# A three-block sequence kernel: convolution fed in narrower units, the S5 recurrence moved to VectorE, the last section taken token tile by token tile

## The reference, cut to what matters

```
# second block, x: (512, 1024), u = rms_norm(x) * g
a, a_z, b_val, b_gate, b_z = split(u @ ev_w_in)          # each (512, 1024)
# S5: 64 groups of 16 channels, 64 complex states each
s_t = Lbar * s_{t-1} + Bbar u_t ;  y_t = Re(C s_t) + D u_t
ya  = gelu(y);  ya = ya * sigmoid(ya @ w_glu + b) * silu(a_z)
# conformer convolution, 31 taps, causal, depthwise
h   = b_val * sigmoid(b_gate)
h   = silu(layer_norm(conv31(h)))
yb  = (h @ w_pw + b_pw) * silu(b_z)
x   = x + rms_norm([ya, yb] @ ev_w_out)
# third block (GLA), end of it
y   = sum over 4 heads of o_h @ od_w_out[h]              # (512, 1024)
out = x + rms_norm(y)
```

## Time and profile before

| | |
|---|---|
| median of 3 runs | 1820.9 us (1819.47 to 1821.16) |
| profiled execution, its own time | 1818.73 us |
| span in the profile | 1817.0 us |
| TensorE (PE) busy | 1680.5 us, 92% |
| VectorE (DVE) busy | 1005.8 us, 55% |
| ScalarE (ACT) busy | 610.4 us, 34% |
| GpSimd (POOL) busy | 296.3 us, 16% |
| mean granted TensorE clock | 0.969 |

### The profile page before, as it was taken

The page is one execution under the profiler, slowest core; times in us unless marked ns, Lnnn a source line. Parts: engine busy times, 40 slices in busy tenths (PEclk is TensorE's granted clock), DMA queues, the critical chain, the costliest instruction groups (busy, mean ns, idle before and its releaser), DMA issues.

```text
span 1817.0 us, 20356 instructions
## 1 busy us (share of the span) xinstructions
PE 1680.5 (92%) x7876; PEld 1364.0 (75%) x7876; DVE 1005.8 (55%) x1271; ACT 610.4 (34%) x852; POOL 296.3 (16%) x316
## 2 busy tenths in 40 slices
PE   6999989999999999989977876999989999999995
PEld 5887878878888888879955656768877777787764
DVE  4375254552345244547999979965454344354434
ACT  4333322233212233343411214255245244243431
POOL 4980000000000000030199284200000000000000
PEclk9999999999999999999988898999999999999998
DMA  8556433233333322263312231115313122131211
GB/s 243 131 146 161 118 103 94 93 116 109 100 93 98 100 93 99 76 232 93 117 35 58 70 139 47 47 64 170 105 47 93 59 82 92 46 105 57 70 47 58
DMA packets 129467, 177.39 MB, mean 98 GB/s; under 512 B 50683, under 2 KB 61419, under 8 KB 128363
## 3 DMA queue, kind: packets, MB, share of 16 engines
q1 hardware_dynamic: 127563, 173.62, 30.9%
q10 hardware_dynamic: 1664, 2.13, 0.4%
q0 software_dynamic: 160, 0.52, 0.2%
HBM read 161.58 MB, written 14.68 MB: 97 GB/s over the span
## 4 chain that ended last, share of the span: by engine, by line
PE 76%; DVE 19%; ACT 2%; issue 1%; POOL 1%; SPq 0%; DMA 0%; ACTq 0%; DVEq 0%; POOLq 0%
PE PS L1960 67%; DVE TMP L1639 8%; DVE WL L1295 2%; PE PS L1938 2%; PE PS L2210 1%; PE PS L2228 1%; DVE FIX L1676 1%; DVE S L1678 1%; PE PS L2081 1%; PE PS L2219 1%; ACT XN L901 1%; DVE V L1373 1%; DVE SEGV L1610 1%; DVE S L1621 1%; DVE S L1618 1%
## 5 line engine op out<-in xcount | busy, mean ns | idle before, releaser
L1960 PE MATMUL PS<-HH,WH 128*128 128x512 f32 x1216 | 485.4, 399 | 46.5 <-DVE WL L1295 35.5
L1295 DVE TENSOR_TENSOR WL<-WR,WH 128x1024 fp32r<-128x1024 f32 x200 | 256.3, 1289 | 466.3 <-ACT WH L896 466.2
L1960 PE MATMUL PS<-HL,WH 128*128 128x512 f32 x1216 | 479.8, 395 | 0.0
L1960 PE MATMUL PS<-HH,WL 128*128 128x512 f32 x1216 | 479.3, 394 | 0.0
L896 ACT ACTIVATE WH<-WR 128x1024 fp32r<-128x1024 f32 x200 | 210.7, 1059 | 709.1 <-PE PS L1960 695.7
L1960 PEld LDWEIGHTS PS<-HH,WH 128*128 128x128 f32 x1216 | 232.6, 191 | 103.0 <-DVE WL L1295 30.7
L1960 PEld LDWEIGHTS PS<-HL,WH 128*128 128x128 f32 x1216 | 232.9, 192 | 49.1 <-issue 1.0
L1960 PEld LDWEIGHTS PS<-HH,WL 128*128 128x128 f32 x1216 | 232.3, 191 | 49.6
L1639 DVE SCALAR_TENSOR_TENSOR TMP<-CP,PRM,TMP 128x512 f32<-128x512 f32 x232 | 183.7, 838 | 0.0
L1960 PE MATMUL PS<-WH,HH 128*128 128x512 f32 x384 | 152.6, 397 | 6.5 <-DVE WL L1295 4.2
L1960 PE MATMUL PS<-WH,HL 128*128 128x512 f32 x384 | 151.6, 395 | 0.0
(11 more groups left out here) (312 smaller groups left out, 2039.3 us busy)
## 6 DMA issues: line engine op xcount, KB each, us to landing
WR<-in_w_in_dram SPq DMA_DIRECT2D x96, 512.0 KB, 3.7
WR<-in_ev_w_in_dram SPq DMA_DIRECT2D x40, 512.0 KB, 3.6
WR<-in_od_w_in_dram SPq DMA_DIRECT2D x32, 512.0 KB, 3.9
WR<-in_ev_w_out_dram SPq DMA_DIRECT2D x16, 512.0 KB, 3.6
WR<-in_od_w_in_dram SPq DMA_DIRECT2D x32, 256.0 KB, 3.3
WR<-in_od_w_out_dram SPq DMA_DIRECT2D x16, 512.0 KB, 3.8
WR<-in_w_branch_a_dram SPq DMA_DIRECT2D x8, 512.0 KB, 3.6
WR<-in_w_branch_b_dram SPq DMA_DIRECT2D x8, 512.0 KB, 3.6
```

Of the source, the lines that this page charges most:

```text
L1295: dve.tensor_tensor(WL[:, s, :, :], WR[:, s, :, :], WH[:, s, :, :].bitcast(F32), ALU.subtract).then_inc(w_lo, 1)
L1960: mm = pe.matmul(out_banks[m], st, mv, start=(kt == 0 and i == 0), stop=(kt == 2 * per - 1 and i == 2))
```

## The change

The units `b_val.0`, `b_gate.0`, `b_val.1`, `b_gate.1` become `b_vg.0` to `b_vg.3`, each with the values and gates of 256 channels (two channel tiles). Their chunks are loaded by two DMAs of 256 columns. Taps start after `b_vg.0`. POOL's loop, carries and corrections go; VectorE runs the whole recurrence (`recurrence`), now between weight splits by a budget of microseconds instead of between taps, and the taps it displaces come later. `mean` moves behind `ev_a.0`. The last head takes its output by token tile, both halves of a tile before the next, and norm and output follow each tile. In all heads RR and OL alternate.

```diff
-PP = PAIRS - 8
+FIX_BLOCKS = PAIRS // FB
...
-_add("b_val.0", 4, 0, 4)
-_add("b_gate.0", 4, 0, 4)
+_add("b_vg.0", 4, 0, 4)
+_add("b_vg.1", 4, 0, 4)
...
+_add("ev_a.0", 4, 0, 4)
 _add("mean", side=1, d=1)
-_add("ev_a.0", 4, 0, 4)
+_add("ev_a.1", 4, 0, 4)
 _add("var", a=1)
-_add("ev_a.1", 4, 0, 4)
...
+                if n in PAIRED:
+                    for b in range(2):
+                        sp.dma_start(WR[:, slot, :, 256 * b:256 * b + 256],
+                                     src[:, D * b:D * b + 256].rearrange("(k p) n -> p k n", p=P)).then_inc(w_loaded[slot], 16)
+                    return
...
-            with pool.Fori(0, SEG_CH - 1) as j:
...
-            for n, (b, ri) in enumerate(FIX_POOL):
...
+            def value_gate(i):
+                evac(f"b_vg.{i}", [CP[:, 2 * i + m, CPAD:] for m in range(2)], ACT.Copy)
+                via_tmp(f"b_vg.{i}", ACT.Sigmoid, GATEV, range(2, 4))
...
             split()
-            split()
-            times_tmp([("b_gate.0", m, CP[:, m, CPAD:]) for m in range(4)], GATEV)
+            gate_value(0)
...
+            def recurrence():
+                sv = S[:, :, :, :].rearrange("p r g (s j) -> p r g s j", j=SEG_CH)
+                shape = [P, 2, PAIRS, SEG]
...
+                    first = seq.inc(dve.tensor_tensor(w1, LAM[:, 0:1, :].unsqueeze(3).to_broadcast(shape), now, ALU.mult))
+                    yield 0.69
+                    second = seq.inc(dve.tensor_tensor(w2, LAM[:, 1:3, :].unsqueeze(3).to_broadcast(shape), now, ALU.mult))
+                    yield 0.69
                     seq.wait(first)
+                    third = seq.inc(dve.tensor_tensor(nxt, nxt, w1, ALU.add))
+                    yield 0.69
+                    seq.wait(third)
                     seq.inc(dve.tensor_tensor(nxt[:, 1:2], nxt[:, 1:2], w2[:, 0:1], ALU.add))
+                    yield 0.43
+                    last = seq.inc(dve.tensor_tensor(nxt[:, 0:1], nxt[:, 0:1], w2[:, 1:2], ALU.add))
+                    yield 0.43
...
+                for g in range(1, SEG):
...
+                for b in range(FIX_BLOCKS):
...
+            def split_recur(states, us):
+                for q in range(4):
+                    spent = 0.0
+                    while spent < us:
+                        spent += next(states, us)
+                    split(1)
+
+            split_convolve(24)
+            gate_value(1)
             split_convolve(24)
             split_convolve(24)
-            convolve(44)
-            steps = step_ops()
-            split_convolve(20, steps)
-            split_convolve(12, steps)
...
+            convolve(16)
+            s5 = recurrence()
+            split_recur(s5, 4.2)
+            gate_value(2)
+            split_recur(s5, 3.8)
+            gate_value(3)
+            split_recur(s5, 3.8)
+            split_recur(s5, 4.2)
+            split_recur(s5, 4.2)
+            for _ in s5:
                 pass
...
             split()
             convolve(24)
...
             split_convolve(24)
-            convolve(len(todo))
             for u in range(2):
                 if u:
-                    split()
+                    split_convolve(16)
                     h_low(3, lambda kt: YA[:, kt, :], range(4))
...
             h_low(3, lambda kt: YA[:, kt, :], range(4, 8))
+            split_convolve(20)
+            convolve(len(todo))
             done("mean")
...
-                for m in range(4):
-                    dve.wait_ge(ot_out, h * 4 + (m + 1))
-                    dve.tensor_tensor(RR[:, m, :], A[m], RR[:, m, :], ALU.mult).then_inc(o_f, 1)
-                for m in range(4):
-                    dve.wait_ge(o_hi, h * 4 + (m + 1))
...
+                for m in range(5):
+                    if m < 4:
+                        dve.wait_ge(ot_out, h * 4 + (m + 1))
+                        dve.tensor_tensor(RR[:, m, :], A[m], RR[:, m, :], ALU.mult).then_inc(o_f, 1)
+                    if m:
+                        dve.wait_ge(o_hi, h * 4 + m)
+                        dve.tensor_tensor(OL[:, m - 1, :], RR[:, m - 1, :], OH[:, m - 1, :].bitcast(F32), ALU.subtract).then_inc(o_lo, 1)
...
+            def last_add(t, u):
+                dve.wait_ge(halves_done, 2 * t + u + 1)
+                dve.tensor_tensor(YO2[:, t, u * NC:(u + 1) * NC], (B, A)[u][t], YO2[:, t, u * NC:(u + 1) * NC],
+                                  ALU.add).then_inc(y2_half, 1)
+
+            def weigh(t, u):
...
+            def last_norm(t):
+                dve.wait_ge(std5, t + 1)
+                seq.inc(dve.reciprocal(STAT[:, 3, t:t + 1], STAT[:, 0, t:t + 1]))
+                seq.wait()
+                dve.wait_ge(yg_done, 2 * t + 2)
+                dve.scalar_tensor_tensor(YO2[:, t, :], YG2[:, t, :], STAT[:, 3, t:t + 1], X1[:, t, :], ALU.mult, ALU.add).then_inc(fin, 1)
+
             for t in range(TT):
...
+                last_add(t, 0)
+                if t == 0:
+                    dve.wait_ge(prow1_in, 16)
+                weigh(t, 0)
+                last_add(t, 1)
+                weigh(t, 1)
+                last_norm(t)
...
+            section("ev_a", H, ready(h_lo, 3), rows=True, units=(0,))
             pe.wait_ge(ones_in, 1)
             pe.wait_ge(conv_done, 8)
             free("mean")
...
+            def out_by_tile(n0, acts, kt_ready):
...
+                for kt in range(4):
+                    kt_ready(kt)
+                    for u in range(2):
...
+                        step(0, u, kt)
+                for t in range(1, TT):
+                    for u in range(2):
+                        for kt in range(4):
+                            step(t, u, kt)
```

More of the change, by code:

```diff
@@ L119 @@
     _add(f"s5_z.{_i}", side=1, a=4)
[L120 to L121 removed]
+_add("b_vg.2", 4, 0, 4)
+_add("b_vg.3", 4, 0, 4)
 _section("a_z2", a=4)
@@ L172, with transfers @@
 N_STATIC = _sum(1, len(JOBS))
+PAIRED = {chunks_before(f"b_vg.{i}") + q for i in range(4) for q in range(4)}
+def transfers(n, since=0):
+    return sum(2 if m in PAIRED else 1 for m in range(n % RING, n + 1, RING) if m >= since)
 HEAD_CHUNKS = 16
@@ L1159, in _ @@
             ya_halves(range(4, 8))
+            split()
+            act.wait_ge(h_lo, 32)
+            evac("ev_a.0", [YO[:, m, 0:NC] for m in range(4)], ACT.Copy)
             for kt in range(KT):
@@ L1344, in times_tmp, with gate_value @@
                     state["via"] += 1
+            def gate_value(i):
+                times_tmp([(f"b_vg.{i}", 2 + m, CP[:, 2 * i + m, CPAD:]) for m in range(2)], GATEV)
             for t in range(TT):
@@ L1604, in step_ops @@
                         seq.wait(last)
-                    seq.inc(dve.tensor_tensor(w1, LAM[:, 0:1, PP:].unsqueeze(3).to_broadcast(shape), now, ALU.mult))
-                    first = seq.n
-                    yield
-                    if last:
-                        seq.wait(last)
-                    seq.inc(dve.tensor_tensor(w2, LAM[:, 1:3, PP:].unsqueeze(3).to_broadcast(shape), now, ALU.mult))
-                    second = seq.n
-                    yield
+                    first = seq.inc(dve.tensor_tensor(w1, LAM[:, 0:1, :].unsqueeze(3).to_broadcast(shape), now, ALU.mult))
@@ new lines, in recurrence @@
+                seq.wait(last)
+                dve.memset(BNA[:, 0, 0:1], 0.0).then_inc(carried, 1)
+                used = [last, last]
+                for b in range(FIX_BLOCKS):
+                    for q in range(2):
+                        made = []
+                        for ri in range(2):
+                            fix, into, by, end, op = correction(b, ri, q, ri)
+                            seq.wait(used[ri])
+                            made.append(seq.inc(dve.tensor_tensor(fix, by, end, ALU.mult)))
+                            yield 0.59
+                        for ri in range(2):
+                            fix, into, by, end, op = correction(b, ri, q, ri)
+                            seq.wait(made[ri])
+                            used[ri] = seq.inc(dve.tensor_tensor(into, into, fix, op))
+                            yield 0.59
+                    if b % 4 == 3:
+                        seq.wait(used[1])
+                        dve.memset(BNA[:, 0, 0:1], 0.0).then_inc(fixed, 1)
@@ L1880, in head @@
                 dve.wait_ge(y2_add, h * 8 + 8)
-                for u in range(2):
-                    if u and not last:
+                for u in range(0 if last else 2):
+                    if u:
                         hsplit(n, HEAD_CHUNKS + V_AT, 2)
@@ L2093, in _ @@
             turn_tokens("u_t", XN1, xn1)
-            section("b_val", H, ready(h_lo, 2), units=(0,))
-            section("b_gate", H, ready(h_lo, 2), units=(0,))
+            section("b_vg", H, ready(h_lo, 2), units=(0, 1))
             section("a_in", H, ready(h_lo, 2), rows=True, tok=strided)
@@ L2117, in _ @@
                 mm.then_inc(side_done, 1)
-            section("b_val", H, ready(h_lo, 2), units=(1,))
-            section("b_gate", H, ready(h_lo, 2), units=(1,))
```

(4 more changed lines are left out.)

166 lines of the change are left out of this document (69 added, 97 removed).

## The result

The changed kernel took **1824.9 us** (median of 12 runs, 1822.95 to 1828.52) against 1819.9 for the kernel before, timed beside it (12 runs). The ratio is 1.0031, with an interval of 1.0023 to 1.0040. That is slower by about 5 us, where 16.5 less had been forecast. The profiled execution took 1823.63 us for a span of 1821.9.

A forecast was written before the change was run, and what follows sets the result against it. TensorE, busy 92% of the span, was taken as the bound, with VectorE setting the pace in two stretches and working alone at the end. Gains of 5.3 + 11.2 = 16.5 off 1820.9 gave 1804.4 us, range 1794 to 1815.

The forecast's parts named there:

- Part 1, the recurrence: Recurrence on VectorE, up to the end of `b_z2.1`: step of 4.17 us, lateness 6.2 us, TensorE free at 1034.1.
- The bound from below: Recurrence step on VectorE if operands were contiguous: 2.7 us.
- Part 2, from E to `mean`: From the end of `b_z2.1` to `mean`: `mean` starts at E + 157.9, TensorE idle some 47 us before it.
- E: Time at which TensorE is free at the end of `b_z2.1`: 1034.1 forecast, 1027.9 without lateness.
- Part 3, `ev_a.0` ahead of `mean`: From `mean` to `pw`: `pw` starts at M + 47.1; gain 11.5 less 6.2 of lateness, 5.3 us.
- M: Time at which `mean` starts, put at E + 157.9.
- Part 4, the last section: End of the kernel, output and norm by token tile: last pass ends at 1802.7 instead of 1813.9, gain 11.2 us.
- The rival by which it gains half: Last section: VectorE held over 1 us more per tile falls behind TensorE, ends 5 us later, 1809; chance 0.12.
- slower than before: Recurrence on one engine becomes the bound: gain gone at a 5.3 us step, 1831 at 6 us; chance 0.04.
- Steps at the contiguous rate: Recurrence steps run at the rate of contiguous operands: no lateness, gain 22.7 us, 1798.2; chance 0.30.
- `mean` came 2.2 us late: Rival on the taps and YL loop before `mean`: ten us of further waits make 1814; chance 0.09.
- about 10 us idle before `pw`: Sign in the new trace: TensorE idles about 10 us before `pw`, as `ev_a.1` no longer covers the chain behind `var`.

The follow-up runs named there:

- e7: The change with SyncE loading pw's chunks ahead of its wait for var, X1 and LWR, and recurrence steps on neighbouring elements of S instead of 64 bytes apart: 1802.0 us.
- e1: The changed kernel with one edit: SyncE loads the chunks of pw ahead of its wait for var, of X1 and of LWR: 1805.4 us.
- e4: The kernel before with only the new last section and the alternation of RR and OL: 1806.6 us, ratio 0.9925.
- e5: The changed kernel with mean back ahead of ev_a.0 and var ahead of ev_a.1, splits and ScalarE's order to match: 1809.4 us.
- e6: The change with pw's chunks loaded first and 26 taps moved earlier, 12 before the recurrence and 14 before the low halves of YL: 1788.2 us.
- e9: e6 with 6 more taps moved earlier and 24 taps interleaved with the four splits ahead of them: 1786.1 us, ratio 0.9815.

## Why the prediction was wrong

**The sign was wrong, and the time outside the range**: 1824.9 against 1804.4, with 0.04 for slower. Point by point:

*Part 1, the recurrence: right.* The step took 4.26 us where I had 4.17, and TensorE waited 4.8 us (0.21 + 1.59 + 2.98) for splits, where I had 6.2. I had put the wait at the second chunk of `a_z2.1`; it came at the last two chunks of `a_z2.0` and the first of `a_z2.1`. POOL was still from 900 to `glu`. The bound from below was exact too: 2.72 measured in e7, 2.7 in the text. Choosing the nearest row (same line, same stride) was the right choice between the two. This is also where the rule of the Trainium skill, Advanced Engine Details and Errata, section SBUF Cachelines (a different cacheline at each access costs speed), spoke against the move: the trace agrees, with 1051 ns at a step of 64 bytes and 684 for neighbours (e1 and e7, L1585); but the price was paid in 3.4 us, not in the whole gain.

*Part 2, from E to `mean`: right in the sum, in part by luck.* E was 1037.1 (1040.23 - 3.15) instead of 1034.1, and `mean` started 157.2 us behind it, against 157.9 forecast. It began at 1194.24 instead of 1192.0, with 47.15 us idle in front of it, against 47. Of the 3.0 us at E, 1.8 stood in the trace before the recurrence (the transposes of AS, at 880.68 in the kernel before, are at 882.45), the shorter waits took 1.4 off, and TensorE ran from 969 to 977 us, behind the wait of 2.98, at a granted clock of 0.79, which is 1.7. The 0.9 left over is the restart behind the three waits: a chunk behind a wait takes some 0.3 more than 5.44 (953.64 to 959.38 is 5.74). That `mean` is met so well behind E hides two errors that cancel. VectorE ended its YL loop at E + 46.3 where I had E + 49.2: `s5_y` ran at the full granted clock (1.00 from 1040 to 1046), while the rows that I took its length from began at 0.74 and 0.73. From there to `mean` it took 110.9 instead of 108.7, of which two waits of 0.90 for ScalarE's copies are 1.8.

*Part 3, `ev_a.0` ahead of `mean`: the step that failed.* It put `pw` at M + 47.1, from `mean`, `ev_a.1`, `var` "with what follows it to the first YL". That last term, 16.7 us, was read from the trace of before. There ScalarE goes to the root straight from the copies of `ev_a.0`, and SyncE loads the chunks of `pw` while TensorE does `ev_a.1`. I carried the duration over without asking which queue entries stand in it once the order is new. Two were changed by the diff or by the move: SyncE's `wait_ge(sq_used, KT)`, now behind a later `var` and still ahead of `pw`'s loads, and ScalarE's `split()`, now ahead of the root. I had priced TensorE and VectorE at the moved jobs, ScalarE's order not at all, and SyncE only for its 32 smaller DMAs. Measured: M + 66.7 in the change, M + 48.0 in e1 (1241.73 - 1193.76), where the 0.9 above my 47.1 is `mean` itself, 9.51 us instead of 8.60, since TensorE starts it at half clock and stays there longer. e1, without those 18.75 us, comes to 1805.4, 1.0 above the forecast; but 1804.4 was counted from 1820.9, and e1's own kernel before took 1819.4, so its gain is 14.0 of the 16.5.

*Part 4, the last section: right.* 11.4 us in the change and 11.2 in e4, against 11.2. The last pass ends at 1818.82, 3.3 us behind the last matmul (1793.47 + 22.04 = 1815.5), with 3.5 forecast; the terms that I listed come to 3.3, and I had added them up to 3.5. The rival by which it gains half did not come: VectorE waits 0.82 us for TensorE in the last two tiles, so it keeps up.

*The rivals:* "slower than before" was tied to one mechanism, a step beyond 5.3 us; the kernel became slower by another, that stood in none. Steps at the contiguous rate did not come (1.05 us and not 0.68), and `mean` came 2.2 us late, not 10. What I had listed as signs of being wrong (TensorE waiting through all of `b_z2`, an early `mean`, a late last tile) did not appear; "about 10 us idle before `pw`" did fail, at 28.55, and that one line of the trace leads to the cause.

*Open:* the kernels with the change begin the S5 part 0.7 to 3.0 us later than the kernel before (0.1 in e4), 0.2 of it at the first matmul and 1.4 in the change by 230 us, where the diff changes nothing that TensorE does. The traces place it in the first 30 us: the first 32 transposes take 5.90 us in the change and 5.11 before, and between 26 and 28 us the granted clock is 0.50 in the change and 0.89 before. Why is not known, and no run was made on it. It is part of what e1's gain lacks.

## What to carry to other kernels

When a job is moved on one engine, go through every queue for waits that name that job, and ask what is issued behind each of them. Here the DMA queue waited for `var` on behalf of one buffer and held back eight transfers that had nothing to do with it. A duration read across several engines ("from `var` to the first YL") holds only as long as the order of each engine inside it does: where the diff touches that order, take the term apart before you carry it over. When TensorE waits for a late instruction, follow the releaser back past the engine named: VectorE, ScalarE, the DMA, SyncE's wait, four steps to the line that costs 19 us.

## What the runs showed of the hardware

- **Stride on VectorE** (e1 and e7). Steps of 64 bytes against neighbouring fp32 elements cost 1051 against 684 ns for a product of 512 elements, and 626 against 425 for an add of 256. That is 0.7 to 0.8 ns an element more at either length. Carried on from 64 and 128 elements the forecast had 0.99 for the product, 1.11 for the large add (measured 1.10) and 0.62 for the small one.
- **The clock behind a long wait.** The stretches of PE in the changed kernel, around the wait for `mean`:

```profile
...
core 0: us, PE busy (x), PEclk, DMA share, GB/s
...
1170.00:1194.00 24.00, 0.00 (x0) 0.50 0.00 0
1194.00:1198.00 4.00, 3.76 (x5) 0.50 0.00 0
1198.00:1203.00 5.00, 5.00 (x11) 0.89 0.00 0
1203.00:1225.00 22.00, 22.00 (x97) 1.00 0.00 1
...
```

TensorE begins `mean` at half clock (1.2 GHz), with nothing done for 47 us, and is back at 2.4 within 9 us. The 16 matmuls of `mean` take 9.51 us; the 16 of the same shape in `var`, at a granted clock of 1.00, take 7.03. So the wait of 47 us costs 2.5 us on top of itself. It was no more behind a longer wait: after 70.44 us (e5) `mean` takes 9.36, and after 5.92 us, in the kernel before, 8.60 (granted clock 0.63 from 1184 to 1188). Making such a gap shorter is worth what it is shortened by, as e6 and e9 show; the 2.5 us come back only if the clock stays up, which no run here shows for `mean`.
